# Addresses of buffers in a two-layer trunk kernel: five columns fewer of set-up results, h and what lies above it 32 bytes lower, the second network's f 64 bytes above the first's

## The chip, the core and the metric

The kernel runs on one core of a Trainium2 chip. The metric is the time of one execution in microseconds (us) on that core; lower is better. A time is the median of several runs. The profile comes from one further execution, with a time of its own.

## What is computed

The reference is a trunk of two layers on an input of 512 tokens by 1024 features, in float32. Cut to what matters here:

```python
# layer 0
h = rms_norm(x, norm_mix[0])
x = x + diff_mla_mixer(h, ...)          # 4 differential heads, 8 latent heads, one output projection
h = rms_norm(x, norm_ffn[0])
x = x + (silu(h @ w_gate[0]) * (h @ w_up[0])) @ w_down[0]     # D_FF = 2816
# layer 1
h = rms_norm(x, norm_mix[1])
x = x + stick_breaking_mixer(h, ...)    # 16 heads of 64
h = rms_norm(x, norm_ffn[1])
x = x + (silu(h @ w_gate[1]) * (h @ w_up[1])) @ w_down[1]
```

## The kernel before, in words

All tensors lie transposed, features on the 128 partitions and 512 tokens along the free dimension. Every float32 operand of a large product is kept as a pair, a rounded high part and the remainder as a low part (`h_hi`, `h_lo`, `w_hi`, `w_lo`, `f_hi`, `f_lo`), and each product is three matmuls: high by high, low by high, high by low. The matmuls of one 128x512 output tile accumulate in one PSUM bank.

Weights come in 180 chunks of 128 partitions. SyncE starts the DMA of a chunk into one of three slots of `wraw`, ScalarE copies it to `w_hi` (`split_hi`, L317), GpSimd subtracts to get `w_lo` (`split_lo`, L329), and TensorE uses it in `project` (L341 and L342 for the two products with `w_hi`, L345 for the one with `w_lo`). In these three lines the weights are the stationary operand and a 512-column row of h, f or mixed is the moving one. In the lines of the attention that read h with w (L666 to L679 and L929 to L933), h is stationary and the weights are moving. A name such as `bank<-h_hi,w_hi` in a row has the moving operand first.

The order of the program is: latents and projections of layer 0, eight latent heads and four differential heads, the output projection, network 0 (`ffn_pe`, `ffn_act`, `ffn_dve` with L=0), the norm and 16 stick-breaking heads of layer 1 in eight pairs, its output projection, network 1 (L=1). A network runs two halves; a half is 22 gate and up chunks of 24 matmuls each, then eight down chunks of 33 matmuls each, whose moving operand is f. The order on each engine is written out by hand, and engines meet at semaphores only.

The buffers are placed by hand too. `place` (L145) rounds an offset up to a multiple of 32 bytes and either goes on from a cursor or takes an address. The cursor starts at byte 16,512 of a partition, and in order come `x`, `wraw`, `w_hi`, `w_lo`, the identity and ones (`mat`), `ident_r`, `cmask`, `vec` (42 columns), `tiny` (T_N = 549 columns of small results, L99 to L127), `rstd`, `h_hi`, `h_lo`, and at `phase0` what the phases share: the attention's buffers, or f with `fy`, `fs`, `fu`, `fa` (L236 to L241), or the buffers of the stick-breaking heads from `c0` (L244) on. All sizes except those of `vec` and `tiny` are multiples of 128 bytes. So `x`, `wraw`, `w_hi`, `w_lo`, `ident_r` and `cmask` start on multiples of 64 bytes, `tiny` too, and `tiny` takes 549 x 4 = 2196 bytes, rounded up to 2208; `rstd`, h, f and everything else above it start 32 bytes past a multiple of 64. There is one f for both networks.

`T_LP`, `T_LE` and `T_LD` (L118 to L120) hold steps of the one scalar of the differential attention, worked out in the set-up; its result goes to `T_NLAM`. `T_RHO` and `T_L0` (L116, L117) are written per head in the differential attention, from L1205 on, and L1205 reads `T_NLAM`. `sqn` and `ssum` (L231, L232) hold the squares of a norm and their sum.

Of the kernel before, what the change touches and what calls it, by code (L numbers as in the profile page):

```python
# [39 lines left out]
F32 = mybir.dt.float32  # L40
F32R = mybir.dt.float32r
ALU = mybir.AluOpType
ACT = mybir.ActivationFunctionType
AX = mybir.AxisListType.X

P = 128
D = 1024
SEQ = 512
# [14 lines left out]
HALF_F = D_FF // P // 2  # L63
# [51 lines left out]
T_R = 524  # L115
T_RHO = 528  # L116
T_L0 = 532  # L117
T_LP = 536  # L118
T_LE = 538
T_LD = 540  # L120
T_BQ = 541
T_EPS = 542
T_EQ = 543
T_NLAM = 547
T_OG = 548
Z_B = (Z_B0, Z_B1)
T_N = 549  # L127


def width_of(g):  # L130
# [10 lines left out]
def trunk(nc, xt, w_ab, w_in, w_down, mats, masks_a, masks_c, tabs, rows, vecs, out):  # L141
# [3 lines left out]
    def place(name, shape, dt, at=None):  # L145
        size = 4 * int(np.prod(shape[1:]))
        off = cursor[0] if at is None else at
        off = (off + 31) // 32 * 32
        t = nc.alloc_sbuf_tensor_at(name, list(shape), dt, offset=off)
        if at is None:  # L150
            cursor[0] = off + size
        return t, off + size

    def pair(name, shape, at=None):
        a, end = place(name + "_hi", shape, F32R, at)
        b, end = place(name + "_lo", shape, F32R, None if at is None else end)
        return (a, b), end
# [70 lines left out]
    on, end = place("on", [P, SEQ], F32, at=end)  # L228
    osq, end = place("osq", [P, SEQ], F32, at=end)

    sqn, end = place("sqn", [P, 2, SEQ], F32, at=vb0)  # L231
    ssum, _ = place("ssum", [P, SEQ], F32, at=end)  # L232
    zeros = ptlo


    (fhi, flo), end = pair("f", [P, HALF_F, SEQ], at=phase0)  # L236
    fy, end = place("fy", [P, SEQ], F32, at=end)
    fs, end = place("fs", [P, SEQ], F32, at=end)
    fu, end = place("fu", [P, SEQ], F32, at=end)
    fa, end = place("fa", [P, SEQ], F32, at=end)  # L240
    assert end <= vb0, (end, vb0)  # L241


    c0 = phase0 + 2 * 4 * KT * SEQ  # L244
# [23 lines left out]
    def S(name):  # L268
        if name not in sems:
            sems[name] = nc.alloc_semaphore(name)  # L270
        return sems[name]
# [11 lines left out]
    def tile_at(t, k, rows=slice(0, P)):  # L283

        return t[rows, k, :] if isinstance(k, int) else t[rows, bass.ds(k, 1), :]
# [5 lines left out]
    def as3(ap, k):  # L291

        return ap if isinstance(k, int) else ap.rearrange("p (o n) -> p o n", o=1)
# [220 lines left out]
    def ffn_pe(pe, L, n):  # L514
        g_first = (G_FFN0, G_FFN1)[L]
        for s in range(2):
            g0 = g_first + s * FFN_HALF

            def gate_up(f, j):
                for c in range(2):  # L520
                    g = f * 2 + (g0 + c)
                    sl = slot(g0 + 2 * j + c)

                    if isinstance(f, int):
                        if s or f >= 3:
                            pe.wait_ge(*at_net(L, "yu"[c], s * HALF_F + f - 2 if f >= 3 else HALF_F))
                    elif s:
                        pe.wait_ge(*at_net(L, "yu"[c], f + (HALF_F - 2)))
                    project(pe, g, sl, bank[2 * j + c][:], h_hi, h_lo)
            if s == 0:  # L530

                for f in range(3):
                    for c in range(2):
                        g = g0 + 2 * f + c
                        project(pe, g, slot(g), bank[2 * f + c][:], h_hi, h_lo,
                                need_h(pe, n) if f == 0 and c == 0 else None)
                        if f == 0:
                            if c == 0:
                                norm_pe(pe, n, 7)
                            else:  # L540
                                rs_spread_pe(pe, f"n{n}", 7)
                with pe.Fori(1, GU_LOOP // 3) as i:
                    for j in range(3):
                        for c in range(2):
                            pe.wait_ge(*at_net(L, "yu"[c], i * 3 + (j - 2)))
                            project(pe, i * 6 + (g0 + 2 * j + c), slot(g0 + 2 * j + c),
                                    bank[2 * j + c][:], h_hi, h_lo)
                for f in range(GU_LOOP, HALF_F):
                    gate_up(f, f % 3)
            else:  # L550
                pe.wait_ge(*at_net(L, "x", 6))
                with pe.Fori(0, GU_LOOP // 3) as i:
                    for j in range(3):
                        for c in range(2):

                            pe.wait_ge(*at_net(L, "yu"[c], i * 3 + (j - 2 + HALF_F)))
                            project(pe, i * 6 + (g0 + 2 * j + c), slot(g0 + 2 * j + c),
                                    bank[2 * j + c][:], h_hi, h_lo)
                for f in range(GU_LOOP, HALF_F):
                    gate_up(f, f % 3)  # L560
            gd = g0 + 2 * HALF_F
            f_hi = [fhi[:, k, :] for k in range(HALF_F)]
            f_lo = [flo[:, k, :] for k in range(HALF_F)]

            def need_f(kt):
                pe.wait_ge(*at_net(L, "lo", s * HALF_F + kt + 1))
            down_banks = (6, 7, 0)
            for d in range(3):
                if s:
                    pe.wait_ge(*at_net(L, "x", KT))  # L570
                project(pe, gd + d, slot(gd + d), bank[down_banks[d]][:], f_hi, f_lo,
                        need_f if d == 0 else None)
            for d in range(3, KT):
                pe.wait_ge(*at_net(L, "x", s * KT + d - 2))
                project(pe, gd + d, slot(gd + d), bank[down_banks[d % 3]][:], f_hi, f_lo)

    def ffn_act(act, L, n_next):
        g_first = (G_FFN0, G_FFN1)[L]
        for s in range(2):
            g0 = g_first + s * FFN_HALF  # L580

            def tile(i, j):
                f = i * 3 + j

                def split_ahead(c):

                    g = g0 + 2 * j + c
                    split_hi(act, i * 6 + g, slot(g), i * 2 + (g // WSLOTS + 1),
                             width_of(i * 6 + g) if isinstance(i, int) else W_IN)
                act.wait_ge(*at_net(L, "y", f + (s * HALF_F + 1)))  # L590
                nc.scalar.activation(fs[:], fy[:], ACT.Silu).then_inc(S("net_s"), 1)  # L591

                split_ahead(3)
                act.wait_ge(*at_net(L, "a", f + (s * HALF_F + 1)))
                nc.scalar.activation(tile_at(fhi, f), as3(fa[:], f), ACT.Copy).then_inc(S("net_hi"), 1)  # L595
                split_ahead(4)
            with act.Fori(0, GU_LOOP // 3) as i:
                for j in range(3):
                    tile(i, j)
            for f in range(GU_LOOP, HALF_F):  # L600
                tile(GU_LOOP // 3, f - GU_LOOP)
            for d in range(KT):
                act.wait_ge(*at_net(L, "x", s * KT + d + 1))
                if s and n_next is not None:
                    norm_act(act, n_next, d)
                hi_static(act, g0 + 2 * HALF_F + d + 3)

    def ffn_dve(dve, L, n, n_next):
        g_first = (G_FFN0, G_FFN1)[L]
        norm_rstd_dve(dve, n, 7)  # L610
        for s in range(2):
            g0 = g_first + s * FFN_HALF

            def tile(f, j):
                dve.wait_ge(S("chunk_done"), f * 2 + (g0 + 1))
                nc.vector.tensor_tensor(fy[:], bank[2 * j][:], rstd[:], ALU.mult).then_inc(S("net_y"), 1)  # L616
                dve.wait_ge(S("chunk_done"), f * 2 + (g0 + 2))
                nc.vector.tensor_tensor(fu[:], bank[2 * j + 1][:], rstd[:], ALU.mult).then_inc(S("net_u"), 1)  # L618
                dve.wait_ge(*at_net(L, "u", f + (s * HALF_F + 1)))
                dve.wait_ge(*at_net(L, "s", f + (s * HALF_F + 1)))  # L620
                nc.vector.tensor_tensor(fa[:], fu[:], fs[:], ALU.mult).then_inc(S("net_a"), 1)  # L621
                dve.wait_ge(*at_net(L, "hi", f + (s * HALF_F + 1)))
                nc.vector.tensor_tensor(tile_at(flo, f), as3(fa[:], f), tile_at(fhi, f),
                                        ALU.subtract).then_inc(S("net_lo"), 1)
            ffn_each(dve, tile)
            gd = g0 + 2 * HALF_F
            for d in range(KT):
                dve.wait_ge(S("chunk_done"), gd + d + 1)
                if s:
                    dve.wait_ge(*at_net(L, "x", KT))  # L630
                b = bank[(6, 7, 0)[d % 3]]
                nc.vector.tensor_tensor(x[:, d, :], b[:], x[:, d, :], ALU.add).then_inc(S("net_x"), 1)  # L632
                if s and n_next is not None:
                    norm_dve(dve, n_next, d)
# [1650 lines left out]
```

## Time and profile before

| | us |
|---|---|
| median of 3 runs | 1347.8 |
| lowest and highest of the 3 | 1343.21 and 1350.05 |
| profiled execution, its own time | 1350.78 |
| span of the profiled execution | 1349.0 |
| mean granted TensorE clock | 0.985 of full speed |

Engines in the profile: PE is TensorE's matmul, PEld its weight load, DVE is VectorE, ACT is ScalarE, POOL is GpSimd, SP is SyncE. Times are in us unless marked ns. Matmuls are pipelined and their ends are modelled: what one costs in a stream is the distance between two starts.

### The profile page before, as it was taken

To read this page: it belongs to the slowest core of one execution; us is meant where nothing else is said; L and a number is where in the kernel's file an instruction comes from. 1 tells how busy PE (TensorE), PEld (TensorE's weight loads), DVE (VectorE), ACT (ScalarE), POOL (GpSimd) and SP (SyncE) were. 2 spreads that over 40 slices of the span, in tenths; PEclk is the share of its full clock that TensorE was granted. 3 is DMA by queue.
4 is the path that set the end of the run, shared out by engine and by line. 5 is a ranking of instruction groups with operands and counts; after the bars stand their busy time and mean duration, and the time that the engine had idled before them with its cause. 6 is when DMAs were issued, how large, how long until landed. Compare 5 with 4: busy or idle time off the path is not lost.

```text
span 1349.0 us, 16920 instructions
## 1 busy us (share of the span) xinstructions
PE 1297.7 (96%) x6308; PEld 1078.6 (80%) x6308; DVE 600.4 (45%) x1033; ACT 574.6 (43%) x953; POOL 513.1 (38%) x223
## 2 busy tenths in 40 slices
PE   9888898999999999999989999998999999999999
PEld 8788887778888888888868888786888888888887
DVE  8877777753222012222168888877232221122210
ACT  5646575543322122233357767675323321222310
POOL 5432411264444434444522222220744453344441
PEclk9899999999999999999989999998999999999999
DMA  5210111022223222233111111110322232222331
GB/s 205 78 56 33 34 46 32 16 93 91 93 100 124 74 78 93 93 117 102 63 63 47 47 62 47 54 55 16 109 91 95 95 114 90 74 97 94 100 128 39
DMA packets 29143, 105.84 MB, mean 78 GB/s; under 512 B 3360, under 2 KB 3616, under 8 KB 29088
## 3 DMA queue, kind: packets, MB, share of 16 engines
q1 hardware_dynamic: 28944, 105.07, 23.7%
q8 instruction: 37, 0.61, 0.2%
q14 instruction: 18, 0.15, 0.0%
q10 hardware_dynamic: 144, 0.02, 0.0%
HBM read 102.98 MB, written 2.10 MB: 78 GB/s over the span
## 4 chain that ended last, share of the span: by engine, by line
PE 67%; DVE 17%; ACT 10%; issue 5%; POOL 1%; DMA 0%; ACTq 0%; DVEq 0%; POOLq 0%
PE bank L341 20%; PE bank L342 19%; PE bank L345 19%; DVE cs_hi L1476 2%; DVE cs_lo L1478 1%; ACT ca L1434 1%; ACT w_hi L317 1%; ACT ca L1432 1%; ACT cq_hi L1515 1%; DVE pt_lo L1079 1%; POOL ssum L435 1%; DVE tiny L399 1%; PE bank L929 1%; ACT pn L1065 1%; PE bank L933 1%
## 5 line engine op out<-in xcount | busy, mean ns | idle before, releaser
L329 POOL TENSOR_TENSOR w_lo<-wraw,w_hi 128x1024 fp32r<-128x1024 f32 (+4 forms) x180 | 457.4, 2542 | 766.7 <-ACT w_hi L317 766.6
L341 PE MATMUL bank<-h_hi,w_hi 128*128 128x512 f32 x896 | 357.3, 399 | 0.7 <-DVE h_lo L425 0.7
L342 PE MATMUL bank<-h_lo,w_hi 128*128 128x512 f32 x896 | 355.0, 396 | 0.0
L317 ACT ACTIVATE w_hi<-wraw 128x1024 fp32r<-128x1024 f32 (+4 forms) x180 | 197.3, 1096 | 159.7 <-DVE x L632 130.2
L345 PE MATMUL bank<-h_hi,w_lo 128*128 128x512 f32 x896 | 227.0, 395 | 0.0
L341 PEld LDWEIGHTS bank<-h_hi,w_hi 128*128 128x128 f32 x896 | 169.1, 189 | 42.0 <-DVE h_lo L425 1.2
L342 PEld LDWEIGHTS bank<-h_lo,w_hi 128*128 128x128 f32 x896 | 169.1, 189 | 39.9
L345 PEld LDWEIGHTS bank<-h_hi,w_lo 128*128 128x128 f32 x896 | 168.2, 188 | 41.0
L341 PE MATMUL bank<-f_hi,w_hi 128*128 128x512 f32 x352 | 139.1, 395 | 0.0
L342 PE MATMUL bank<-f_lo,w_hi 128*128 128x512 f32 x352 | 139.0, 395 | 0.0
L618 DVE TENSOR_TENSOR fu<-bank,rstd 128x512 f32<-128x512 f32 x44 | 30.4, 692 | 205.0 <-PE bank L345 205.0
L632 DVE TENSOR_TENSOR x<-bank,x 128x512 f32<-128x512 f32 x32 | 22.1, 692 | 205.0 <-PE bank L345 205.0
L595 ACT ACTIVATE f_hi<-fa 128x512 f32 (+1 forms) x44 | 27.8, 632 | 200.2 <-DVE fa L621 200.2
L591 ACT ACTIVATE fs<-fy 128x512 f32<-128x512 f32 x44 | 27.8, 633 | 143.3 <-DVE fy L616 143.3
L345 PE MATMUL bank<-f_hi,w_lo 128*128 128x512 f32 x352 | 87.3, 395 | 0.0
L345 PEld LDWEIGHTS bank<-f_hi,w_lo 128*128 128x128 f32 x352 | 66.1, 188 | 16.1
L342 PEld LDWEIGHTS bank<-f_lo,w_hi 128*128 128x128 f32 x352 | 66.1, 188 | 16.1
L341 PEld LDWEIGHTS bank<-f_hi,w_hi 128*128 128x128 f32 x352 | 66.1, 188 | 16.0
L616 DVE TENSOR_TENSOR fy<-bank,rstd 128x512 f32<-128x512 f32 x44 | 30.4, 691 | 108.9 <-PE bank L345 108.4
L929 PE MATMUL bank<-w_hi,h_hi 128*128 128x256 f32 x192 | 58.0, 302 | 5.1 <-DVE ka L965 4.7
L933 PE MATMUL bank<-w_lo,h_hi 128*128 128x256 f32 x192 | 56.0, 292 | 0.0
L931 PE MATMUL bank<-w_hi,h_lo 128*128 128x256 f32 x192 | 55.9, 291 | 0.0
(272 smaller groups left out, 2021.1 us busy)
## 6 DMA issues: line engine op xcount, KB each, us to landing
wraw<-in_w_in SPq DMA_DIRECT2D x120, 512.0 KB, 3.3
wraw<-in_w_down SPq DMA_DIRECT2D x32, 704.0 KB, 4.1
wraw<-in_w_ab SPq DMA_DIRECT2D x20, 512.0 KB, 3.3
x<-in_xt SPq DMA_DIRECT2D x8, 256.0 KB, 5.9
out<-x SPq DMA_DIRECT2D x8, 256.0 KB, 2.0
wraw<-in_w_ab SPq DMA_DIRECT2D x4, 416.0 KB, 5.9
wraw<-in_w_ab SPq DMA_DIRECT2D x2, 384.0 KB, 3.0
wraw<-in_w_ab SPq DMA_DIRECT2D x2, 256.0 KB, 2.8
```

The costliest lines, as they stand in the source:

```text
L317: nc.scalar.activation(whi[:, s, 0:width], wraw[:, s, 0:width], ACT.Copy).then_inc(S("w_hi"), 1)
L329: nc.gpsimd.tensor_tensor(wlo[:, s, 0:width], wraw[:, s, 0:width], whi[:, s, 0:width], ALU.subtract).then_inc(S("w_lo"), 1)
L341: nc.tensor.matmul(out_bank, w, src_hi[kt], start=(kt == 0), stop=False)
L342: nc.tensor.matmul(out_bank, w, src_lo[kt], start=False, stop=False)
L345: last = nc.tensor.matmul(out_bank, wlo[:, s, kt * P:(kt + 1) * P], src_hi[kt], start=False, stop=(kt == n - 1))
L591: nc.scalar.activation(fs[:], fy[:], ACT.Silu).then_inc(S("net_s"), 1)
L595: nc.scalar.activation(tile_at(fhi, f), as3(fa[:], f), ACT.Copy).then_inc(S("net_hi"), 1)
L616: nc.vector.tensor_tensor(fy[:], bank[2 * j][:], rstd[:], ALU.mult).then_inc(S("net_y"), 1)
L618: nc.vector.tensor_tensor(fu[:], bank[2 * j + 1][:], rstd[:], ALU.mult).then_inc(S("net_u"), 1)
L929: nc.tensor.matmul(o, tok(hhi, 4 * c + k, i), whi[:, slot(g), w], start=(c == 0 and k == 0 and i % 2 == 0), stop=False, skip_group_check=True)
L931: nc.tensor.matmul(o, tok(hlo, 4 * c + k, i), whi[:, slot(g), w], start=False, stop=False, skip_group_check=True)
L933: last = nc.tensor.matmul(o, tok(hhi, 4 * c + k, i), wlo[:, slot(g), w], start=False, stop=(c == 1 and k == 3), skip_group_check=True)
```

## The change

It alters addresses only: no instruction, wait, shape or order. The first hunk lets `T_LP` and `T_LE` use the four columns of `T_RHO` and `T_LD` the first of `T_L0`, so `tiny` has 544 columns, 2176 bytes, a multiple of 64, and everything placed after it lies 32 bytes lower. The second gives each network an f of its own, in nearly the same place: the first at `phase0`, the second 64 bytes above. `fy`, `fs`, `fu` and `fa` follow the second one, so they lie 64 bytes higher against `phase0`. `sqn` and `ssum` start 512 bytes higher, since `fa` now reaches 64 bytes past `vb0`. The other hunks use the f of the network at hand.

```diff
-T_LP = 536
-T_LE = 538
-T_LD = 540
-T_BQ = 541
-T_EPS = 542
-T_EQ = 543
-T_NLAM = 547
-T_OG = 548
+T_LP = T_RHO
+T_LE = T_RHO + 2
+T_LD = T_L0
+T_BQ = 536
+T_EPS = 537
+T_EQ = 538
+T_NLAM = 542
+T_OG = 543
 Z_B = (Z_B0, Z_B1)
-T_N = 549
+T_N = 544
...
-    sqn, end = place("sqn", [P, 2, SEQ], F32, at=vb0)
+    sqn, end = place("sqn", [P, 2, SEQ], F32, at=vb0 + 512)
...
-    (fhi, flo), end = pair("f", [P, HALF_F, SEQ], at=phase0)
+    f_of = (pair("f0", [P, HALF_F, SEQ], at=phase0)[0], pair("f1", [P, HALF_F, SEQ], at=phase0 + 64)[0])
+    end = phase0 + 64 + 2 * 4 * HALF_F * SEQ
...
-            f_hi = [fhi[:, k, :] for k in range(HALF_F)]
-            f_lo = [flo[:, k, :] for k in range(HALF_F)]
+            f_hi = [f_of[L][0][:, k, :] for k in range(HALF_F)]
+            f_lo = [f_of[L][1][:, k, :] for k in range(HALF_F)]
...
-                nc.scalar.activation(tile_at(fhi, f), as3(fa[:], f), ACT.Copy).then_inc(S("net_hi"), 1)
+                nc.scalar.activation(tile_at(f_of[L][0], f), as3(fa[:], f), ACT.Copy).then_inc(S("net_hi"), 1)
...
-                nc.vector.tensor_tensor(tile_at(flo, f), as3(fa[:], f), tile_at(fhi, f),
+                nc.vector.tensor_tensor(tile_at(f_of[L][1], f), as3(fa[:], f), tile_at(f_of[L][0], f),
```

## Rows read from the trace of the kernel before

**Rows 1.** Page: the span, and busy time of each engine.

```profile
span 1349.0 us, 16920 instructions
...
PE 1297.7 (96%) x6308; PEld 1078.6 (80%) x6308; DVE 600.4 (45%) x1033; ACT 574.6 (43%) x953; POOL 513.1 (38%) x223
```

**Rows 2.** Page: granted TensorE clock in 40 slices, tenths of full speed.

```profile
PEclk9899999999999999999989999998999999999999
```

**Rows 3.** Page: the chain that ended last, share by engine.

```profile
PE 67%; DVE 17%; ACT 10%; issue 5%; POOL 1%; DMA 0%; ACTq 0%; DVEq 0%; POOLq 0%
```

**Rows 4.** Chain in order of time: start, length, piece; both networks.

```profile
353.28 1.86 PE bank L345 x8
358.88 1.86 PE bank L345 x8
...
1335.55 2.57 PE bank L345 x11
1343.24 2.58 PE bank L345 x11
```

**Rows 5.** PE groups by form: operands, count, busy us, mean ns, idle before.

```profile
L345 PE MATMUL bank<-h_hi,w_lo 128*128 128x512 f32 x896 | 227.0, 395 | 0.0
L342 PE MATMUL bank<-f_lo,w_hi 128*128 128x512 f32 x352 | 139.0, 395 | 0.0
...
L819 PE MATMUL bank<-w_lo,kvl_hi 128*128 128x512 f32 x8 | 3.2, 395 | 0.0
```

**Rows 6.** Timeline of PE at 50 us: start, length, line, operands.

```profile
50.24 0.39 PE L818 MATMUL bank<-w_hi,kvl_lo 128*128 128x512 f32 x1
...
51.87 0.40 PE L819 MATMUL bank<-w_lo,kvl_hi 128*128 128x512 f32 x1
```

**Rows 7.** Timeline of PE at 153 us.

```profile
152.68 0.28 PE L1036 MATMUL bank<-bk_hi,bq_hi 96*128 96x256 f32 x1
...
153.04 0.28 PE L1038 MATMUL bank<-cmask,ident_r 128*128 128x256 f32 x1
153.16 0.28 PE L1036 MATMUL bank<-bk_hi,bq_hi 96*128 96x256 f32 x1
```

**Rows 8.** Timeline of PE at 14 and at 19 us.

```profile
13.96 0.35 PE L666 MATMUL bank<-w_hi,h_hi 128*128 128x416 f32 x1
...
15.12 0.93 PE L671 MATMUL bank<-w_lo,h_hi 128*128 128x416 f32 x4
...
19.05 0.35 PE L666 MATMUL bank<-w_hi,h_hi 128*128 128x416 f32 x1
...
20.17 0.91 PE L671 MATMUL bank<-w_lo,h_hi 128*128 128x416 f32 x4
```

**Rows 9.** Timeline of PE at 146 us, in a stretch at half clock.

```profile
146.26 0.41 PE L931 MATMUL bank<-w_hi,h_lo 128*128 128x256 f32 x1
146.47 0.41 PE L933 MATMUL bank<-w_lo,h_hi 128*128 128x256 f32 x1
```

**Rows 10.** DVE groups by form, columns as in rows 5.

```profile
L618 DVE TENSOR_TENSOR fu<-bank,rstd 128x512 f32<-128x512 f32 x44 | 30.4, 692 | 205.0 <-PE bank L345 205.0
...
L632 DVE TENSOR_TENSOR x<-bank,x 128x512 f32<-128x512 f32 x32 | 22.1, 692 | 205.0 <-PE bank L345 205.0
```

**Rows 11.** ACT groups by form.

```profile
L317 ACT ACTIVATE w_hi<-wraw 128x1024 fp32r<-128x1024 f32 x140 | 146.9, 1049 | 68.7 <-DVE x L632 39.2 <-DVE cyv L1503 26.6 <-PE bank L1327 2.4
L317 ACT ACTIVATE w_hi<-wraw 128x1408 fp32r<-128x1408 f32 x32 | 43.9, 1373 | 91.0 <-DVE x L632 91.0
L591 ACT ACTIVATE fs<-fy 128x512 f32<-128x512 f32 x44 | 27.8, 633 | 143.3 <-DVE fy L616 143.3
```

**Rows 12.** POOL groups by form.

```profile
L329 POOL TENSOR_TENSOR w_lo<-wraw,w_hi 128x1024 fp32r<-128x1024 f32 x140 | 339.4, 2425 | 638.8 <-ACT w_hi L317 638.8
...
L973 POOL TENSOR_TENSOR ka<-ka,t 128x1024 f32<-128x1024 f32 x2 | 5.1, 2558 | 0.0
```

More of the change, by code:

```diff
@@ L240, in trunk @@
     fa, end = place("fa", [P, SEQ], F32, at=end)
-    assert end <= vb0, (end, vb0)
+    assert end <= vb0 + 512
     c0 = phase0 + 2 * 4 * KT * SEQ
```

## The prediction, made before the changed kernel was run

> **What bounds the kernel now.** I read the page first: of a span of 1349.0 us TensorE is busy for 1297.7, and no other engine for more than half of it [rows 1]. A busy PE in this profile needn't be PE at its peak, so I went on to the chain that ended last: 67% of it is PE, 17% DVE, 10% ACT [rows 3]. In order of time it shows what a chunk costs in the networks: the last eight matmuls of neighbouring gate chunks start at 353.28 and 358.88, so 24 matmuls take 5.60 us, 233.3 ns each; the last eleven of two down chunks start at 1335.55 and 1343.24, so 33 matmuls take 7.69 us, 233.0 ns each [rows 4]. That pace is the same in both networks, with three engines busy beside it or, at the end, with hardly any. The groups say that nothing stands ahead of these matmuls: no idle time before L342 and L345 [rows 5]. So in the networks, in the stick-breaking projections and in the output projections the kernel is a stream of 512-column matmuls. Their number: 44 gate and up chunks in each of the two networks and 24 for q, k and v, times 24 matmuls, is 2688; 32 down chunks times 33 is 1056; two output projections of 8 chunks times 24 is 384; in all 4128. At 233.3 ns they take 963 us of the 1349. The rest, some 386 us, is attention, where DVE, ACT and shorter matmuls share the chain.
>
> At the full clock of 2.4 GHz, 512 columns last 213.3 ns. Each matmul thus has 20.0 ns on top, and an address is one thing on which those could hang. The whole question of this change is whether they do: 4128 x 20.0 ns is 83 us.
>
> **The change, part by part.** It has no instruction, wait or DMA more or less, so nothing queues anew on any engine. What it changes is the phase of addresses, by which I mean the remainder by 64 bytes. Before, weights, x, `ident_r` and `cmask` have phase 0, and h, f, mixed and all other buffers above `tiny` have 32. After, all have phase 0. By 128 bytes, weights stay at 0, h and the first f go from 96 to 64, the second f goes from 96 to 0.
>
> *The matmuls.* The trace of before holds three of the four pairings of phases. Moving 32 on stationary 0 is h and f on weights: 233.3 ns. Moving 0 on stationary 32 is L817 to L819, weights moving over `kvl`: seven starts lie between 50.24 and 51.87 us, 232.9 ns each [rows 6], and the modelled length is 395 ns, as for h and f [rows 5]. The moving weights there also lie on multiples of 128. Moving 32 on stationary 32 is L1036 on `bq` and `bk`, at 256 columns: three starts in 0.36 us, 120 ns each [rows 7]. The fourth pairing, 0 on 0, is what all 4128 become. Of that the trace has one sample, and at 256 columns only: L1038, `cmask` on `ident_r`, whose start lies 0.12 us ahead of the next, like those of its neighbours of pairing 32 on 32 [rows 7]. So phase 0 of either operand alone changes nothing at 512 columns, and both together change nothing at 256. I take 0 ns for each matmul, from the nearest rows. Both ends: the timeline has matmuls of 416 columns with the same operands at two paces. Six starts from 13.96 to 15.12 make 193.3 ns each; six from 19.05 to 20.17 make 186.7 [rows 8]. So the added time goes in steps, and one step is 6.67 ns. I take one step in either direction as the bound of what a change of phase can do: 4128 x 6.67 ns = 27.5 us less or more. For the second f alone it is 528 x 6.67 = 3.5 us.
>
> That the 20 ns hang on an address at all has a row against it. In a stretch at half clock, 256 columns take 0.21 us from start to start [rows 9], which is 256 / 1.2 GHz with nothing on top; at full clock 256 columns take 0.12 [rows 7], against 0.107 for 256 / 2.4 GHz. What is added shows at the full clock alone, though the operands lie where they lie.
>
> The Trainium skill bears on this in "TensorE: Matmul & The Clock Gate", section "Wait — 56ns, not 53.3ns?": it gives 215.7 ns from start to start for 512 columns at full clock. The trace has 233.3, so by that page 17.6 ns of each matmul would be avoidable, and if these addresses were the cause, 4128 x 17.6 = 73 us would go. The rows in which one operand already has phase 0 keep the longer distance, so this trace speaks against addresses as its cause.
>
> *DVE.* Reading and writing x, at phase 0, and reading `rstd` for `fu`, at 32, take the same 692 ns for the same shape [rows 10]. Cost and gain 0; I see no bound but a rounding of 1 ns.
>
> *ACT.* A copy at phase 0 takes 1049 ns for 1024 columns and 1373 for 1408, which is 0.844 ns a column and by this 617 ns for 512 columns; `fs<-fy` at phase 32 takes 633 [rows 11]. The functions differ, which accounts for 16 ns easily, so I take 0. If it were all phase, ACT's share of the chain, 10% or 135 us, would shrink by 16/633, 3.4 us.
>
> *POOL.* w_lo at phase 0 takes 2425 ns, `ka` at phase 32 takes 2558, and there are only two of the latter [rows 12]. With 1% of the chain on POOL [rows 3], 13 us, 5% of that is 0.7 us. I take 0.
>
> *Shared columns.* `T_LP`, `T_LE` and `T_LD` are dead once `T_NLAM` is written, and the instruction that first writes `T_RHO` reads `T_NLAM`. So no wait is needed and none is added. `sqn` moved by 512 bytes keeps its phase. Both 0.
>
> *The sum.* The profiled execution: 1349.0 + 0 = 1349.0 us of span, 1350.8 as its own time, 3.0 above the median of the three runs. The forecast for the median is the median of before, 1347.8.
>
> **The rivals.**
>
> A, faster by a step. When both operands start on a multiple of 64, each of the 4128 matmuls loses one step of 6.67 ns: 1347.8 - 27.5 = 1320. For it: the pairing is absent at 512 columns, and steps exist [rows 8]. Against it: the one sample at 256 columns, and the fact that the same operands, at the same phases, show both paces [rows 8], so that something other than the phase picks the step.
>
> B, the whole excess goes: 1347.8 - 83 = 1265. (By the page's figure named above it would be 1275.) Against it are the rows of pairings that already have one operand at phase 0 [rows 5, 6].
>
> C, slower. A weight load runs beside nearly every matmul: PEld is busy for 1078.6 us within PE's 1297.7 [rows 1]. Before, the moving row and the weights being loaded differ in phase by 32 bytes, and after they have the same. If two reads of the same phase at once get in each other's way, every matmul takes one step more: 1347.8 + 27.5 = 1375. It decides from 6.7 us on, which is 1.6 ns for each matmul. Against it: L1036, with both operands at phase 32, and L1038, both at 0, go at the pace of the rest [rows 7]. The Trainium skill, "SBUF — State Buffer", section "Who interferes with whom", has it that TensorE's reads of the moving operand and of the weights go through ports of their own; by that C would give nothing, and no row here shows the ports.
>
> **How the numbers follow.** A measurement of this kernel can tell some 0.5% from no change, 6.7 us. Forecast (no effect of the phase): 0.80. A: 0.09. B: 0.02. C: 0.09. Within the forecast stand the small bounds of ACT and POOL, at most 4.1 us less, 3.5 us more for the second f, and the scatter. For the scatter I take half the distance between lowest and highest of the three runs, 6.84 / 2 = 3.4 us; where the half-clock stretches fall (three of the 40 slices are below 9 [rows 2]) may differ from one execution to the next. Range: 1347.8 - 4.1 - 3.4 = 1340, and 1347.8 + 3.5 + 3.4 = 1355. It leaves out A, B and C, 0.20 together. Of the forecast's 0.80 I give 0.02 to faster by over 0.5% and 0.01 to slower. So faster 0.02 + 0.09 + 0.02 = 0.13, slower 0.01 + 0.09 = 0.10, within 0.77.
>
> **What would show it.** Right: L345 pieces 5.60 us apart in a gate chunk, 7.70 in a down chunk, in both networks; L618, L632 and L591 at 692, 692 and 633 ns; the same engine shares of the chain. A shows as 5.44 and 7.48, C as 5.76 and 7.92. If only the second network's down chunks leave 7.70, the second f is the cause, and 528 matmuls are concerned. What would make me wrong is an effect of the pairing 0 on 0, or of 128 bytes, at 512 columns, which the trace of before can't show, since it has no such matmul.

## The result and the profile after

The changed kernel takes 1335.45 us (median of 4 runs, 1334.30 to 1336.34) against 1347.14 us (4 runs, 1343.21 to 1350.05) for the kernel before. The ratio is 0.9901, with a 95% interval of 0.9887 to 0.9914: faster by 1.0%. The forecast was 1347.8 with a range down to 1340, so the gain of nearly 12 us lies outside it.

The page of the changed kernel: span, busy time of each engine, and the chain that ended last. The count of instructions is that of before [rows 1], and the shares of the chain are within one point of those of before: PE has 66% instead of 67% [rows 3].

```profile
span 1334.5 us, 16920 instructions
...
PE 1281.6 (96%) x6308; PEld 1076.2 (81%) x6308; DVE 598.0 (45%) x1033; ACT 574.6 (43%) x953; POOL 514.0 (39%) x223
...
PE 66%; DVE 17%; ACT 10%; issue 5%; POOL 1%; DMA 0%; ACTq 0%; DVEq 0%; SPq 0%; POOLq 0%
```

From L237 on, lines of the kernel stand one further down; L345 of before is L346. The groups by form show what moved, against [rows 5, 10, 11]: matmuls of h are modelled 4 ns shorter and those of f 2 ns. DVE, ACT and POOL stand where they stood.

```profile
L346 PE MATMUL bank<-h_hi,w_lo 128*128 128x512 f32 x896 | 223.4, 391 | 0.0
L346 PE MATMUL bank<-f_hi,w_lo 128*128 128x512 f32 x352 | 86.4, 393 | 0.0
...
L619 DVE TENSOR_TENSOR fu<-bank,rstd 128x512 f32<-128x512 f32 x44 | 30.4, 691 | 200.3 <-PE bank L346 200.3
...
L318 ACT ACTIVATE w_hi<-wraw 128x1024 fp32r<-128x1024 f32 x140 | 146.9, 1050 | 68.2 <-DVE x L633 38.7 <-DVE cyv L1504 26.7 <-PE bank L1328 2.4
...
L330 POOL TENSOR_TENSOR w_lo<-wraw,w_hi 128x1024 fp32r<-128x1024 f32 x140 | 340.0, 2430 | 624.7 <-ACT w_hi L318 624.7
```

The chain in order of time (start, length, piece) gives the distances between starts, to be read beside [rows 4]: gate chunks in the first network, down chunks in the first, down chunks in the second.

```profile
350.79 1.83 PE bank L346 x8
356.28 1.83 PE bank L346 x8
...
431.13 2.52 PE bank L346 x11
438.68 2.52 PE bank L346 x11
...
1100.58 2.56 PE bank L346 x11
1108.25 2.55 PE bank L346 x11
```

A gate chunk takes 5.49 us in place of 5.60, which is 228.9 ns a matmul. A down chunk of the first network takes 7.55 us (228.9 ns), one of the second, whose f lies 64 bytes higher, 7.67 us (232.4 ns). Before, all had 233.3 ns.

Where the time went, by the starts of the first matmul of each stage in the two timelines (my subtraction):

```
stage                               before us   after us   change
up to the first network's 2nd chunk    301.4      300.4     -1.0
first network                          367.2      359.7     -7.5
stick-breaking heads                   259.8      258.9     -0.9
output projection                       45.9       45.9      0.0
second network, to its last matmul     371.1      366.1     -5.0
```

That is 14.4 of the 14.5 us by which the spans differ. The networks alone give 12.5. (The output projection is counted from where its matmuls run on without the heads; 18 of its 192 matmuls come earlier, among the last heads.)

Not all of it is the pace. In the first network the trace of before has 4.8 us at half clock and the changed kernel's has 3.4, which is worth 0.7 of the 7.5 us (my estimate, half of the difference).

In the stick-breaking heads 576 matmuls became 4.4 ns faster, which would be 2.6 us. Next to nothing of it arrives: from the first of these matmuls to the first of the output projection it is 242.6 us before and 242.5 after, so the gain goes into waits. The rest of the 0.9 lies in the piece behind, the 18 early matmuls and the last heads, 17.3 against 16.4 us, where the trace of before has 3.4 us at half clock and the changed kernel's has none. In the twelve traces of this case that piece takes 17.2 to 17.3 us in the nine with such a stretch in it and 16.4 in the three without, whatever the distance, so it is the clock's.

The output projection gained nothing although its matmuls changed like the others; the last section comes back to that.

### The profile page after: what moved, and what is told of

It reads as the page before. It is cut to its first block, busy times and chain, and to the rows that moved or that the text cites. A ratio compares the mean times of both kernels' runs of the same rounds, so it can differ in the third digit from the quotient of the medians.

```text
span 1334.5 us, 16920 instructions
## 1 busy us (share of the span) xinstructions
PE 1281.6 (96%) x6308; PEld 1076.2 (81%) x6308; DVE 598.0 (45%) x1033; ACT 574.6 (43%) x953; POOL 514.0 (39%) x223
## 4 chain that ended last, share of the span: by engine, by line
PE 66%; DVE 17%; ACT 10%; issue 5%; POOL 1%; DMA 0%; ACTq 0%; DVEq 0%; SPq 0%; POOLq 0%
PE bank L342 19%; PE bank L343 19%; PE bank L346 19%; DVE cs_hi L1477 2%; DVE cs_lo L1479 2%; ACT ca L1435 1%; ACT ca L1433 1%; ACT w_hi L318 1%; ACT cq_hi L1516 1%; DVE pt_lo L1080 1%; POOL ssum L436 1%; ACT pn L1066 1%; ACT pn L1054 1%; DVE cs L1445 1%; DVE tiny L1185 1%
## 5 line engine op out<-in xcount | busy, mean ns | idle before, releaser
L346 PE MATMUL bank<-h_hi,w_lo 128*128 128x512 f32 x896 | 223.4, 391 | 0.0
L346 PEld LDWEIGHTS bank<-h_hi,w_lo 128*128 128x128 f32 x896 | 168.3, 188 | 37.0
L346 PE MATMUL bank<-f_hi,w_lo 128*128 128x512 f32 x352 | 86.4, 393 | 0.0
L346 PEld LDWEIGHTS bank<-f_hi,w_lo 128*128 128x128 f32 x352 | 66.2, 188 | 15.0
```

The source lines that it names most:

```text
L346: last = nc.tensor.matmul(out_bank, wlo[:, s, kt * P:(kt + 1) * P], src_hi[kt], start=False, stop=(kt == n - 1))
```

## The experiments

In what follows a distance is the start of the moving row minus the start of the weights, both in bytes within a partition, by a modulus of 256. `w_hi` and `w_lo` start at 128 by 256, their slots and tiles repeat every 512 bytes, and rows of h, f and mixed every 2048, so one distance holds for all matmuls of one operand. Before it is 96 for h, f and mixed. After the change it is 64 for h, mixed and the first f, and 128 for the second f. Expectations that speak of distances by 512 are about the same numbers with one more digit: 320 is 64, 384 is 128.

### Each part alone

First the columns without the second f:

```diff
-    f_of = (pair("f0", ..., at=phase0)[0], pair("f1", [P, HALF_F, SEQ], at=phase0 + 64)[0])
-    end = phase0 + 64 + 2 * 4 * HALF_F * SEQ
+    f_of = (pair("f0", ..., at=phase0)[0], pair("f1", [P, HALF_F, SEQ], at=phase0)[0])
+    end = phase0 + 2 * 4 * HALF_F * SEQ
```

> The first part of the change alone: tiny has 544 columns and both networks use one f at phase0, so h and f all start at 64 by a modulus of 128. Theory 1 (the pace hangs on where the moving row starts) and theory 2 (it hangs on the distance between the moving row and the weights beside it) both expect what the changed kernel shows for h and for the first f, now for the second f too: 24 matmuls in 5.49 us and 33 in 7.55 us in both networks. Against the changed kernel the second network's 16 down chunks gain 16 x (7.67 - 7.55) = 1.9 us, so some 1333.5 us, 1.1% under before. A rival that makes the second f's 64 bytes the cause of a gain expects it slower than the changed kernel.

Measured: 1333.37 us (4 runs), ratio 0.9884 (0.9865 to 0.9902) to a before of 1349.71. The chain now has the second network's down chunks at 7.55 us:

```profile
1100.16 2.52 PE bank L346 x11
1107.71 2.52 PE bank L346 x11
```

Then the second f without the columns: T_N and the numbers of the columns as before, f and `sqn` as in the change. Against the changed kernel:

```diff
-T_LP = T_RHO
-T_LE = T_RHO + 2
-T_LD = T_L0
+T_LP = 536
+T_LE = 538
+T_LD = 540
...
-T_N = 544
+T_N = 549
```

> The second part alone: tiny keeps 549 columns, h and the first f stay at 96 by 128 as before, the second f goes to 32. Both theories expect h at 5.60 us for 24 matmuls and the first f at 7.70 for 33 in the first network, as before. For the second f at 32 neither has a row; if all starts off a multiple of 64 are slow, it stays at 7.70 and the time is that of before, 1347; if it is fast, the gain is at most 16 x 0.15 = 2.4 us, 0.2%.

Measured: 1349.66 us (10 runs), ratio 1.0001 (0.9992 to 1.0011). Gate chunks are back at 5.60 us, and the second f, now at distance 160, is the slowest so far, 7.73 us or 234.3 ns over a whole half:

```profile
340.03 1.86 PE bank L346 x8
345.63 1.86 PE bank L346 x8
...
1110.14 2.58 PE bank L346 x11
1117.87 2.58 PE bank L346 x11
```

So the gain is the columns' alone, and the second f's 64 bytes take a little back: 16 chunks times 0.12 us is 1.9 us, as the chunks show. The two kernels' total times don't tell 1.9 us apart with certainty.

### Where the row starts, or how far it is from the weights?

The expectation below weighs two theories of what sets the pace, where the moving row itself starts (1) or its distance from the weights (2), and a third, that both operands have to be on multiples of 64. The edit puts 32 bytes of padding ahead of the changed kernel's weights:

```diff
+    cursor[0] += 32
     (whi, wlo), _ = pair("w", [P, WSLOTS, W_DOWN])
```

> The changed kernel with 32 bytes of padding ahead of the weights' high part, so that the weights and all above them lie 32 bytes higher. h and the first f are back at 96 by 128, where they were before, the weights are at 32, and the distance between them is that of the changed kernel. Theory 1 (the moving row's own start decides) expects the pace of before: 5.60 us for 24 matmuls, 7.70 for 33 in the first network, some 1347 us. Theory 2 (the distance decides) expects the pace of the changed kernel: 5.49 and 7.55, some 1336 us. A third, that multiples of 64 are what matters for both operands, expects 1347 as well, as both are off them.

Measured: one run of 1334.92 us, and the chain has the pace of the changed kernel everywhere (L347 here is L345 of before):

```profile
337.77 1.83 PE bank L347 x8
343.27 1.83 PE bank L347 x8
...
610.38 2.52 PE bank L347 x11
617.93 2.52 PE bank L347 x11
...
1099.13 2.56 PE bank L347 x11
1106.80 2.55 PE bank L347 x11
```

h and the first f stand at exactly their addresses of before, and neither they nor the weights are on a multiple of 64. Yet the chunks take 5.50, 7.55 and 7.67 us. Theory 1 and the third theory fall; the distance decides. x and `wraw` lie below the padding and didn't move, so the distance of the rows from those is that of before again, and it isn't what counts either.

### All distances

Each half of each network gets an f of its own, at an offset of its own above `phase0`; `sqn` moves up to make room. Three kernels more differ in the four offsets only.

```diff
+    F_HI = (0, 32, 96, 128)
+    f_at = [(place(f"f{n}_hi", [P, HALF_F, SEQ], F32R, at=phase0 + a)[0],
+             place(f"f{n}_lo", [P, HALF_F, SEQ], F32R, at=phase0 + a + b + 4 * HALF_F * SEQ)[0])
+            for n, (a, b) in enumerate(zip(F_HI, F_LO))]
```

> The changed kernel with an f of its own for each half of each network, starting 0, 32, 96 and 128 bytes above phase0, that is at 64, 96, 32 and 64 by 128 (at 448, 480, 32 and 64 by 512); h stays. Each half has 8 down chunks of 33 matmuls. If 128 bytes are the period, the halves take 7.55, 7.70, unknown and 7.55 us for 33 matmuls; if the period is longer, the last differs from the first. If only multiples of 64 matter, the third is 7.70.

> As the sweep before, with the four halves' f 192, 256, 320 and 384 bytes above phase0, so that the distance from the weights' start to the moving row's start is 0, 64, 128 and 192 bytes by 512. So far distances of 320, 352, 384, 416 and 448 gave 228.9, 233.3, 232.4, 234.2 and 233.3 ns a matmul. If the period is 256, a distance of 64 gives 228.9 (7.55 us for 33 matmuls), 128 gives 232.4, 192 gives 233.3; if it is 512, these are unknown; if distances have nothing to do with it and the changed kernel's 64 by 128 was the cause, 320 bytes above phase0 (0 by 128) gives 232.4.

> The same at 160, 224, 288 and 448 bytes above phase0: distances of 480, 32, 96 and 256 by 512. With a period of 256, a distance of 96 gives 233.3 ns and 256 what 0 gives; with one of 512 they are unknown. No theory gives a distance at which the 20 ns above 213.3 vanish, but if one does exist it is among these sixteen.

> The same at 352, 416, 480 and 512 bytes above phase0: distances of 160, 224, 288 and again 320. The last must give the first's 228.9 ns (7.55 us for 33) if 512 bytes hold a whole number of periods, since it is the changed kernel's first f moved by 512 bytes; if it gives another pace, the place itself matters and not the distance by 512.

Two chains, of the second and the third sweep. Second sweep, offsets 192 and 320 (distances 0 and 128):

```profile
431.85 2.49 PE bank L351 x11
439.33 2.49 PE bank L351 x11
...
1099.00 2.55 PE bank L351 x11
1106.66 2.56 PE bank L351 x11
```

Third sweep, offset 448 (distance 0 again, 256 bytes on):

```profile
1283.18 2.49 PE bank L351 x11
1290.66 2.49 PE bank L351 x11
```

The pace of a half is the time between its first and its last start over 263. The four kernels took 1335.38, 1334.98, 1335.51 and 1335.00 us, one run each, too close to tell offsets apart by. By pace, all sixteen offsets and the control at 512, sorted by distance:

```
distance by 256    offsets above phase0    ns a matmul
0                  192, 448                226.9, 226.7
32                 224, 480                233.3, 233.3
64                 0, 256, 512             228.9, 228.9, 228.9
96                 32, 288                 233.4, 233.4
128                64, 320                 232.4, 232.4
160                96, 352                 234.3, 234.3
192                128, 384                233.3, 233.3
224                160, 416                233.3, 233.4
```

(64 is the changed kernel's second f.) Offsets 256 apart agree within 0.2 ns: the period is 256 bytes. A period of 128 falls, since 0 and 128 differ by 5.5 ns. That 512 would be the shortest falls too. The best distance is 0, with 226.7 ns, which is 6.67 ns under the 233.3 of before; none of these eight distances gives 213.3. Both parts of f moved together here, so each distance is one for a whole stream.

### The best distance for all

`vec` and `tiny` move behind `t2`, so `rstd`, h and all above start 2368 bytes lower than in the changed kernel; one f for both networks.

```diff
-    vec, _ = place("vec", [P, V_N], F32)
-    tiny, _ = place("tiny", [P, T_N], F32)
     r0 = cursor[0]
...
     t2, _ = place("t2", [P, 2 * NB * 2 * A_DIM], F32)
+    vec, _ = place("vec", [P, V_N], F32)
+    tiny, _ = place("tiny", [P, T_N], F32)
```

> The kernel with the columns shared and one f, but vec and tiny placed last, behind t2, so that rstd, h, f and mixed start 2368 bytes lower than in the changed kernel: the distance from the weights' start to that of h, f and mixed is 0 by 256 bytes. The sweeps gave 226.7 ns a matmul for f at that distance, 228.9 at 64 and 233.3 at 96. If the distance rules h and mixed as it does f, 24 matmuls take 5.44 us and 33 take 7.48, and all 4128 matmuls of 512 columns save 6.67 ns against before: 27.5 us, some 1320 us, ratio 0.980. If h were ruled by something else that the change also moved, its chunks stay at 5.49 or go back to 5.60.

Measured: 1326.82 us (5 runs, 1326.24 to 1328.49), ratio 0.9831 (0.9817 to 0.9845) to a before of 1350.47. It beats both kernels. Page and chain:

```profile
span 1326.0 us, 16920 instructions
...
PE 1273.7 (96%) x6308; PEld 1078.7 (81%) x6308; DVE 599.9 (45%) x1033; ACT 574.4 (43%) x953; POOL 512.7 (39%) x223
```

```profile
334.82 1.81 PE bank L347 x8
340.26 1.81 PE bank L347 x8
...
430.70 2.49 PE bank L347 x11
438.18 2.49 PE bank L347 x11
```

Chunks are at 5.44 and 7.48 us as expected, yet the span shrank by 23.0 us, not 27.5. The two networks gave theirs: 10.9 us, of which 0.7 are again the shorter stretch at half clock, and 10.4 us, where 3168 matmuls by 6.67 ns are 21.1. The output projection of layer 1 gave 1.0. The heads of layer 1 take 259.5 us, 0.4 less than before, though their matmuls would be good for 3.8: waits take it, as in the changed kernel.

The attention of layer 0 became slower. There the weights are the moving operand and h is loaded, at 256 columns. Taken as everywhere in this text, moving minus loaded, the distance is 0 here, 192 in the changed kernel and 160 before. Over the stages of 36 or 48 such matmuls the timelines give 119.4 to 119.9 ns each at distance 0, 113.4 to 117.8 at 192, and 117 to 119 at 160, pauses and half clock left out. From the first of these matmuls to the output projection of layer 0 it is 172.1 us at distance 0, 171.6 before and 170.7 to 171.1 in five kernels at 192, all with 17.1 us at half clock in between. (The start of the first network's second chunk, 301.2 us against 300.4, doesn't show it by itself: the second sweep, with the changed kernel's addresses up to there, has 301.2 too.) The distance that suits the long matmuls is the worst of three for the short ones.

### Own weights, or the next ones?

The kernel is the one with distance 0, and the padding now stands between the two parts of the weights:

```diff
-    (whi, wlo), _ = pair("w", [P, WSLOTS, W_DOWN])
+    whi, _ = place("w_hi", [P, WSLOTS, W_DOWN], F32R)
+    cursor[0] += 32
+    wlo, _ = place("w_lo", [P, WSLOTS, W_DOWN], F32R)
```

> The kernel of the run before with 32 bytes of padding between the weights' high and low parts: h, f and mixed then lie 0 by 256 from the low part and 32 from the high part. If each matmul's pace hangs on the distance between its own moving row and the weights read beside it, the first 16 matmuls of a gate chunk (high part) go at 233.3 ns and the last 8 (low part) at 226.7: 5.55 us a chunk, and down chunks 22 x 233.3 + 11 x 226.7 = 7.63 us. If the layout as a whole decides, all 24 have one pace.

Measured: one run of 1342.6 us; a gate chunk takes 5.55 us, a down chunk 7.67. The timeline of PE in one gate chunk:

```profile
502.18 1.98 PE L349 MATMUL bank<-h_hi,w_lo 128*128 128x512 f32 x8
504.00 0.39 PE L345 MATMUL bank<-h_hi,w_hi 128*128 128x512 f32 x1
...
507.27 0.39 PE L345 MATMUL bank<-h_hi,w_hi 128*128 128x512 f32 x1
507.50 0.39 PE L346 MATMUL bank<-h_lo,w_hi 128*128 128x512 f32 x1
507.73 1.07 PE L349 MATMUL bank<-h_hi,w_lo 128*128 128x512 f32 x4
```

Fourteen starts from 504.00 to 507.27 make 233.6 ns each; eight from 502.18 to 504.00 make 227.5. The mean over the 22 gate chunks of the first network's second half, from each start to the next, by place in the chunk:

```
matmuls 1 to 15   (weights w_hi, next load w_hi)    233.3 (231 to 235)
matmul 16         (weights w_hi, next load w_lo)    226.7
matmuls 17 to 23  (weights w_lo, next load w_lo)    226.6
matmul 24         (weights w_lo, next load w_hi)    235.0
```

Matmul 16 multiplies by `w_hi`, at distance 32, and is fast; matmul 24 multiplies by `w_lo`, at distance 0, and is slow. In a gate chunk, then, the time up to the next start goes by the next matmul's weights, and in the trace those begin to load 2 to 4 ns after a matmul starts, so beside its moving row. That speaks for a meeting of the two streams, the moving row and the load of the next weights, but doesn't prove it: if a matmul waited ahead of its own start because of its own two operands, the starts would lie the same way. In a down chunk the switch isn't that clean: matmul 22, the last on `w_hi`, still takes 233.4 ns although `w_lo` is loaded beside it, the first seven of the eleven `w_lo` matmuls lie between 224 and 236 ns and only the next three at 226.7. So a chunk takes 7.67 us where 7.63 was expected.

### The high and the low part of f at different distances

The offsets of the first sweep become 0, 0, 192, 192, and the low part is moved a further 192, 32, 64 and 32 bytes (`F_LO`):

```diff
-    F_HI = (0, 32, 96, 128)
-    F_LO = (0, 0, 0, 0)
+    F_HI = (0, 0, 192, 192)
+    F_LO = (192, 32, 64, 32)
```

> The changed kernel with an f of its own for each half, and the low part moved apart from the high part: distances from the weights, by 256, of high and low part are 64 and 0, 64 and 96, 0 and 64, 0 and 32. In the last 11 matmuls of a chunk, whose moving rows are of the high part alone, I expect 228.9, 228.9, 226.7 and 226.7 ns. In the first 22, where rows of both parts alternate, the mean of the two distances' paces if each row counts for itself: 227.8, 231.1, 227.8 and 230.0 ns. If a step is lost only where a row and its neighbour both fit, the alternating ones stay near 233.

Measured: one run of 1337.99 us, and by half, in ns:

```
distances high, low      first 22: expected, measured     last 11: expected, measured
64, 0                    227.8, 231.0                     228.9, 229.8
64, 96                   231.1, 231.9                     228.9, 230.6
0, 64                    227.8, 231.9                     226.7, 228.1
0, 32                    230.0, 231.5                     226.7, 230.5
```

The mean of two paces is not what an alternation gives: even between the two good distances, 0 and 64, it costs 231 to 232. The time of a matmul is therefore not a function of its own distance alone. What its predecessors did seems to carry over, for a few matmuls, as in the down chunks of the experiment before: the last eleven have one moving part and one weight part, and are slower than at the same distance in a uniform stream. How, these runs don't show.

## Why the prediction was wrong

*What bounds the kernel*: right. 4128 matmuls at a fixed pace are the stream on which everything hangs, and a few ns on each made the result.

*No cost elsewhere*: right. DVE and ACT kept their lengths to 1 ns in the groups that I named, POOL to 5 ns of 2425, and the shared columns cost nothing. The bounds that I gave ACT and POOL, 4.1 us, weren't needed.

*The matmuls at 0 ns*: this is the step that failed. I took as the variable the remainder of each operand by 64 bytes, and found three of four pairings at one pace. The variable is the distance between the moving row and the weights, by 256. In these terms my samples were few and unlucky: h and f on weights are at 96, and the weights over `kvl` at 160, both slow in the sweep (233.3 and 234.3) [rows 5, 6]. Equal paces at two distances I read as independence of addresses. `bk` on `bq`, which I used as the pairing 32 on 32, is at distance 0; at 256 columns [rows 7] that distance has no advantage, as the run with all at distance 0 showed, and so it could say nothing about 512. And I overlooked that the trace of before does have this pairing at 512 columns, a little behind the rows that I show:

```profile
154.28 0.39 PE L1036 MATMUL bank<-bk_hi,bq_hi 96*128 96x512 f32 x1
154.51 0.40 PE L1036 MATMUL bank<-bk_lo,bq_hi 96*128 96x512 f32 x1
154.74 0.40 PE L1036 MATMUL bank<-bk_hi,bq_lo 96*128 96x512 f32 x1
154.98 0.28 PE L1038 MATMUL bank<-cmask,ident_r 128*128 128x256 f32 x1
```

The eight triples like this one take 231.4 ns a matmul before, 234.2 in the changed kernel and 227.8 in the one with distance 0, though `bk` and `bq` lie at distance 0 from each other in all three. So these rows wouldn't have warned me: three matmuls between shorter ones don't show the pace that a long stream has at their distance.

I had written that the missing pairing was what could make me wrong, and gave it 0.09; that a matmul could gain up to 6.67 ns was the right size. Where my sum had 0, the changed kernel gains 4.4 ns at distance 64 and 0.9 at 128: 3600 x 4.4 + 528 x 0.9 ns is 16.3 us. The span shows 14.5, since the heads and the output projection of layer 1 lose some 3.3 and the half-clock stretches happen to give back some 1.6. Remainders by 64 couldn't have picked this distance: 192 is a multiple of 64 like it, and goes at 233.3.

*The half clock as evidence*: at 1.2 GHz nothing is on top, whatever the addresses [rows 9]. I took that to speak against addresses. It doesn't: it says that the added time arises at the full clock only, and the later runs show that an address decides a part of it there. At half clock 512 columns take 427 ns at distances of 96, 64 and 0 alike (the second chunk of the first network, before, in the changed kernel and at distance 0).

*Rival A*: its mechanism, both operands on multiples of 64, fell with the padding ahead of the weights, where no operand is on one and the pace stays. Its price was that of the best distance, 6.67 ns on each of 4128 matmuls or 27.5 us. The kernel with distance 0 got 23.0 us of span.

*Rival C*: two reads of the same phase get in each other's way. The direction was wrong, distance 0 is the best. But its picture, a moving row and a weight load that meet, fits the gate chunks of the kernel with `w_lo` moved apart, though it isn't proven, and the down chunks follow it only in part. I had cited the Trainium skill against it. The page "TensorE: Matmul & The Clock Gate", section "Step-by-step: what each phase is for", has it in the same way that loading the next weights takes no read bandwidth from the running matmul, as each has a read port. By that one would expect no effect of the distance, and this case has one: the same stream of matmuls takes 226.7 or 233.3 ns each by how far its rows lie from the weights. Whether the two meet at a port, a bank or in the array isn't shown.

*The figure of 215.7 ns* that the Trainium skill gives for 512 columns at the full clock (the same page, section "Wait — 56ns, not 53.3ns?"), by which 17.6 ns of each would be avoidable: 6.7 of them were, the other 11 stayed at every distance tried.

*One step is 6.67 ns*: the two means of [rows 8] lie that far apart, but single matmuls don't go in such steps, and the changed kernel's mean of 228.9 isn't on one. The last section has what does.

*The range* took only scatter and small bounds beside the 0. For an edit that does nothing but move addresses under 4128 equal matmuls, it should have reached down by the 6.67 ns that I had as the bound.

## What to carry to other kernels

Where a kernel is a stream of equal matmuls, compare the time between starts with columns over clock; if something is left on top, try how far the moving rows lie from the weights, in steps of 32 bytes up to 256: it costs a line of padding. These figures are for 512 columns of this kernel's rounded float32, and other shapes have to be measured. Set it for the longest stream, and look at what the shorter matmuls on the same buffers do, since they may want another distance. When a trace is to show that something doesn't depend on an address, ask first which distances its samples cover. And before a difference of stages is put down to the change, look where the half-clock stretches fell in each.

## What the runs showed of the hardware beyond that

Each distance has a rhythm of its own. At 0 all starts lie 226 or 227 ns apart; at 64 they lie 226, 229 and 232 apart in turn, 686.7 for three; before, at 96, it is 231, 231 and 238, 700 for three. Single matmuls take anything from 225 to 241 ns in these streams, so they don't go in steps. The repeats do: one at 0, two at 192 (466.7), three at 64 and 96, four at 32 (933.3) and seven at 160 (1640) all add up to whole multiples of 6.67 ns, which is 16 columns at 2.4 GHz.

A pace can outlast its cause. In the output projection of layer 1, where mixed is at distance 64, four kernels (the changed one, the columns alone, the weights 32 higher, the low part of f moved apart) had a stretch at half clock within it, and then ran at 233.3 ns to the end of the stage, with the full clock granted; in the changed kernel that is some 38 us, with the first chunk of the network behind. The four sweeps had none within it, and ran at 228.9 ns. The chain has two chunks of this stage, in the changed kernel and in the second sweep:

```profile
935.17 1.87 PE bank L346 x8
940.77 1.87 PE bank L346 x8
```

```profile
934.25 1.83 PE bank L351 x8
939.75 1.83 PE bank L351 x8
```

PE's windows (start and end, length, busy times, granted clock, DMA share, GB/s) in the changed kernel:

```profile
924.00:934.00 10.00, 7.84 (x29) 5.70 (x28) 4.20 (x7) 5.34 (x8) 1.85 (x1) 0.83 0.01 2
940.00:950.00 10.00, 10.00 (x45) 8.09 (x44) 2.70 (x4) 3.19 (x5) 6.43 (x4) 1.00 0.27 88
```

and in the second sweep:

```profile
924.00:934.00 10.00, 7.68 (x35) 5.73 (x34) 4.63 (x7) 4.93 (x8) 1.44 (x1) 1.00 0.01 2
```

The next pause of the stream ends it: the network's second chunk goes at 228.9 again. At distance 0 the same stage, also with a half-clock stretch in it, ran at 226.7. That a stream left by the clock in one rhythm stays in it fits what the alternating distances showed, but no run was made to try it, and the cause is open.
